# Expert slots dealt out over the partitions in steps of eight, and the last pair's gate and up matrices requested whole

## What is computed

```python
def hier_moe(xn, w_router_group, w_router_expert, w_gate, w_up, w_down):
    t = xn.reshape(-1, D_MODEL)                       # 520 tokens x 1024
    ...
    top_v, top_i = lax.top_k(le_g, TOP_K_IN_GROUP)    # 2 of 32 experts for each token
    ...
    def expert_step(acc, ew):
        wg, wu, wd, cw = ew
        h = jax.nn.silu(t @ wg) * (t @ wu)            # 1024 -> 256
        return acc + cw[:, None] * (h @ wd).astype(jnp.float32), None
```

## Time and profile before

| | us |
|---|---|
| median of 3 runs | 596.83 |
| lowest and highest run | 594.62, 599.33 |
| span of the profiled execution | 599.1 |
| PE busy (share of the span) | 550.2 (92%) |
| DVE busy | 278.3 (46%) |
| ACT busy | 168.1 (28%) |
| POOL busy | 158.0 (26%) |
| queue q1, share of the 16 DMA engines' span | 64.1% |
| queue q0, the same | 7.8% |

### The profile page before, as it was taken

One profiled execution on the slowest core, in us unless ns is written; L12 is line 12 of the kernel. 1 busy time (PEld: TensorE's weight loads), 2 busy tenths in 40 slices (PEclk: granted clock), 3 DMA queues, 4 the chain that ended last, 5 costly groups with the idle time before them and its releaser, 6 DMA issues.

```text
span 599.1 us, 8410 instructions
## 1 busy us (share of the span) xinstructions
PE 550.2 (92%) x2970; PEld 321.9 (54%) x2970; DVE 278.3 (46%) x694; ACT 168.1 (28%) x386; POOL 158.0 (26%) x187
## 2 busy tenths in 40 slices
PE   6999999999999988999999999999996968789994
PEld 4798799897765645554555944333332323234321
DVE  5887677978304799623458531121120111111235
ACT  7445343414302656731322210010110000000013
POOL 0488788410001098610000021111120111101003
PEclk9999999999999999999999798999997989989997
DMA  7890342579575930039905759999999999999966
GB/s 279 275 288 30 121 142 83 181 244 312 190 210 174 400 137 3 3 97 383 401 38 185 307 161 369 408 419 419 420 422 421 420 420 420 421 421 421 381 241 249
DMA packets 48215, 163.48 MB, mean 273 GB/s; under 512 B 8674, under 2 KB 22058, under 8 KB 36888
## 3 DMA queue, kind: packets, MB, share of 16 engines
q1 hardware_dynamic: 41360, 144.93, 64.1%
q0 software_dynamic: 6528, 17.01, 7.8%
q10 hardware_dynamic: 288, 1.05, 0.4%
HBM read 151.06 MB, written 19.76 MB: 285 GB/s over the span
## 4 chain that ended last, share of the span: by engine, by line
PE 48%; DMA 16%; SPq 11%; DVE 7%; POOL 3%; issue 3%; ACT 3%; DVEq 0%; POOLq 0%; ACTq 0%
PE bank L1141 10%; DMA ring<-in_w_up_dram 10%; PE bank L1065 9%; SPq L537 7%; PE bank L1168 4%; DMA x<-q_rows 3%; SPq L550 3%; DMA ring<-results 2%; PE bank L1016 2%; PE bank L930 2%; PE bank L813 2%; PE bank L835 2%; POOL ring L2213 2%; PE bank L836 2%; PE bank L840 2%
## 5 line engine op out<-in xcount | busy, mean ns | idle before, releaser
L1141 PE MATMUL bank<-ring,work 128*64 128x512 f32 x512 | 120.6, 626 | 17.7 <-DMA ring<-in_w_up_dram 17.7
L1141 PEld LDWEIGHTS bank<-ring,work 128*64 128x64 f32 x512 | 39.3, 144 | 95.5 <-issue 82.7
L1518 DVE TENSOR_TENSOR work<-work,bank 128x256 f32<-128x256 f32 x16 | 6.7, 422 | 133.7 <-ACT work L1453 133.7
L756 PE MATMUL bank<-split 128*128 128x384 f32 x192 | 66.1, 344 | 0.1
L1168 PE MATMUL bank<-ring,work 128*64 128x512 f32 x256 | 58.5, 598 | 7.6 <-ACT work L1457 7.6
L757 PE MATMUL bank<-split 128*128 128x384 f32 x192 | 64.3, 335 | 0.0
L2280 POOL DMA_INDIRECT work<-hn_rows,tbl x15 | 15.2, 1016 | 106.5 <-PE bank L1151 91.2
L1065 PE MATMUL bank<-ring 128*128 128x512 f32 x96 | 42.9, 596 | 0.0
L1453 ACT ACTIVATE work<-bank 128x256 f32<-128x256 f32 x16 | 6.2, 384 | 129.7 <-PE bank L1141 129.7
L2288 POOL DMA_INDIRECT results<-work,tbl x15 | 15.0, 1001 | 98.8 <-DVE work L2058 98.8
L2213 POOL TENSOR_TENSOR ring<-ring 128x192 f32<-128x192 f32 (+1 forms) x40 | 38.8, 989 | 8.0 <-DVEq L1613 6.8
(11 more groups left out here) (281 smaller groups left out, 878.9 us busy)
## 6 DMA issues: line engine op xcount, KB each, us to landing
ring<-in_w_down_dram SPq DMA_DIRECT2D x32, 1024.0 KB, 25.0
ring<-in_w_gate_dram SPq DMA_DIRECT2D x28, 1024.0 KB
ring<-in_w_up_dram SPq DMA_DIRECT2D x28, 1024.0 KB
ring<-in_w_in_dram SPq DMA_DIRECT2D x7, 1536.0 KB, 11.3
results<-work POOLq DMA_DIRECT2D x1, 4160.0 KB, 24.5
x<-in_x_prompt_dram SPq DMA_DIRECT2D x8, 512.0 KB, 15.8
ring<-in_w_out_dram SPq DMA_DIRECT2D x2, 2048.0 KB
ring<-in_w_gate_dram SPq DMA_DIRECT2D x8, 512.0 KB, 22.3
```

What stands on the lines that cost most here:

```text
L756: pe.matmul(bank[n % 3][:, 0:CW], xT_high[:, k, cols], w_high[c][:, k, :], start=(k == 0), stop=False)
L1141: last = pe.matmul(bank[2][64 * h:64 * h + 64, :], xgT[:, k, 64 * h:64 * h + 64], gate_up[s][h][:, :, k, :], start=(k == 0), stop=(k == KD ...
L1518: return dve.tensor_tensor(out, a, b, op)
```

## The change

The constant becomes `slot_at`: column p holds the number of the slot that lies on partition p. In each half of 64 partitions, slot 0 is on partition 0, slot 1 on partition 8, and so on to slot 7 on partition 56; slot 8 is on partition 1. `in_order` is a view of the same constant that reads 0 to 127 in order, with a stride of eight, for `holder`. The gathered rows, the results and the one-hot matrices follow the table, so all of them change places together.

For the last pair, SP requests the four gate and up matrices whole by `gates`, all counted on `gu_in[0]`, and PE waits once, for all of them, before the first product. The four requests of 1 MB take the place of eight of 512 KB. The order of the requests (gate and up of expert 30, gate and up of expert 31, then the downs) stays that of the other pairs.

```diff
@@ constants
-    seg["iota128"] = np.tile(p[None], (P, 1))
+    seg["slot_at"] = np.tile((p // SL * SL + p % 8 * 8 + p % SL // 8)[None], (P, 1))
@@ build
-        iota128 = cut(rt, 1472, P)
+        slot_at = cut(rt, 1472, P)
+        in_order = slot_at.rearrange("p (h b a) -> p h a b", h=2, b=8)
@@ SP
-            cseg("iota128", iota128).then_inc(S["logc_in"], 16)
+            cseg("slot_at", slot_at).then_inc(S["logc_in"], 16)
...
             sp.wait_ge(S["gu_done"], PAIRS - 3)
-            half_gates((30, 31), 0, 0, S["front_in"])
-            half_gates((30, 31), 0, 1, gu_in[0])
+            gates((30, 31), 0)
             sp.wait_ge(S["dn_done"], PAIRS - 3)
             downs((30, 31), 0)
@@ PE
-            def pair(i, s, turn, first, split=False):
+            def pair(i, s, turn, first):
...
-                pe.wait_ge(*((S["front_in"], 80) if split else (gu_in[s], loads)))
+                pe.wait_ge(gu_in[s], loads)
                 for k in range(KD):
                     if k == KD // 2:
                         pe.wait_ge(S["xg_evac"], 2 * i + 2)
-                        if split:
-                            pe.wait_ge(gu_in[s], loads)
...
-                pair(i, s, i // 3 + 1, False, i == PAIRS - 1)
+                pair(i, s, i // 3 + 1, False)
@@ DVE, pick and place
-                        dve.tensor_scalar(picked[m][0:n, e * SL:(e + 1) * SL], iota128[0:n, 0:SL], place_in[0:n, m, e:e + 1],
+                        dve.tensor_scalar(picked[m][0:n, e * SL:(e + 1) * SL], slot_at[0:n, 0:SL], place_in[0:n, m, e:e + 1],
...
-                        dve.tensor_scalar(in_slot[:, i, m, :], iota128, slot[:, i, m:m + 1], None, ALU.is_equal)\
+                        dve.tensor_scalar(in_slot[:, i, m, :], slot_at, slot[:, i, m:m + 1], None, ALU.is_equal)\
@@ DVE, pair 14
-                        dve.tensor_scalar(holder[:, t, :], iota128, float(t * P), last_token, ALU.add, ALU.is_equal)\
+                        dve.tensor_scalar(holder[:, t, :].rearrange("p (h a b) -> p h a b", h=2, a=8), in_order,
+                                          float(t * P), last_token, ALU.add, ALU.is_equal)\
```

## The result

The changed kernel takes 608.14 us (median of four runs, 606.99 to 610.83) against 597.34 us for the kernel before (594.62 to 599.33). The ratio is 1.0187 with a 95% interval of 1.0143 to 1.0230, that is 8.5 to 13.7 us more. When both were timed again beside two variants (experiment 7), the ratio was 1.0129 (1.0100 to 1.0158). A ratio is computed from all runs of both kernels, so it differs a little from the quotient of the two medians.

The account below looks back on a forecast made before the run. The expert stage was taken as bound by full DMA engines, the one with most rows setting the end. Slots +11.1 and whole requests +0.4 gave +11.5 us, a median of 608.3 us, range 602.5 to 613.5.

Parts of the forecast that it names:

- Dealing B: Which partitions share a DMA engine: runs of four, the run 32 above on the same one, eight per half.
- the sum: From 371.56 to 575.6 us: 180 us of matrices plus the heaviest engine's rows, together 200.9 of 204 us.
- A and C: Other partition-to-engine dealings: A eight neighbours, C partition mod 16; experiment 4 expected -11.5 us for A, +12 for C.
- The slowest DMA engine sets the end: Expert stage: the DMA engine with most rows sets the end, since every matrix is awaited whole; the tail follows.
- Rival M: In experiment 5: half the DMA engines standing idle costs, not the one with most rows; +3 us or less.
- 11.1 us for part 1: Slots in steps of eight: 61 more rows at 0.156 us on the heaviest engine, 9.5, plus 1.6 for earlier rows.
- Part 2 at +0.4 us: Last pair's gate and up matrices requested whole: +0.4 us, range -0.2 to +1.8.
- the slack: Last pair: PE's products end 3.8 us (tile 3: 2.2) before DVE needs them; starting 2.3 late costs 0 to 0.1.
- Line 2078: DVE's strided read, five instructions of 281 ns: covered by PE's work even at twice the time; uncovered, 1.4 us.
- The faster one: Dealing A, blocks of eight neighbours, makes the new layout the even one: -12.6 us, 584 us; chance 0.04.
- Within 1%: Rows slip in beside matrices, or landings depend less on the slowest engine: +0 to +5 us; chance 0.10.
- The dearest case: Rows at 0.172 us (+13.4), PE's low clock in the tail (+1.8) and pair 14 (+1.7): up to 16.9; chance 0.08.

Follow-up runs that it names:

- experiment 7: The changed kernel itself, timed again beside the kernel before: 606.05 against 598.8 us, ratio 1.0129 (1.0100 to 1.0158).
- experiment 4: Changed kernel with slots dealt in steps of four and the last pair's halves kept, against the kernel before: 596.8 against 598.9 us, ratio 0.9952.
- Experiment 5: Changed kernel with halves kept, slots 0 to 7 on one DMA engine of each half, against the kernel before: 607.4 against 598.5 us, ratio 1.0145.
- experiment 2: Changed kernel with the last pair's matrices in halves again, slots still dealt by eight, against the kernel before: 608.5 against 598.9 us, ratio 1.0146.
- experiment 1: Changed kernel with dense slots again, last pair's gate and up still requested whole, against the kernel before: 598.3 against 598.9 us, ratio 0.9995.
- experiment 6: Changed kernel with filler products on PE before the last pair, against the kernel before: 609.0 against 598.8 us, ratio 1.0185.
- run 32: Not a follow-up run and has no time: the run of four partitions lying 32 higher, served by the same DMA engine.
- experiment 3: Changed kernel with halves kept and slots going round the runs of four, against the kernel before: 596.8 against 598.9 us, ratio 0.9954.

## Why the prediction was right, point by point

**Where a row goes: right.** Dealing B, taken from the spread of 12 us, the burst of 14 DMA engines and the sum, holds. The changed kernel's burst at 205 to 226 GB/s and its plateau at 0.5 were foretold by it, and experiment 4 excludes A and C by their sign and size. The first gather's 14 DMA engines came from a single window of 0.2 us, and this reading was a lucky one: the same 15 or 16 DMA engines show only 205 or 144 GB/s in the windows beside it. The packets in flight, 15 and 10, bear it out. The Trainium skill, "DMA: Bandwidth & Descriptors", section "The descriptor swizzle", states this dealing for one 1 MiB transfer to 128 partitions. The runs agree, for gathers and scatters by an index too.

**The slowest DMA engine sets the end: right.** Experiment 5 shows it without eight crowded DMA engines: two crowded ones cost +8.7 us, as eight do in experiment 2. Rival M, lost bandwidth as such, called for 3 us or less.

**11.1 us for part 1: right within the measurement; the price of a row isn't pinned down.** The stretch grew by 11.8 and 13.1 us in the two profiles of the changed kernel and by 10.9 us with halves, for 61 rows more. Divided by the rows of the stretch alone that is 0.18 to 0.21 us per row (10.9 / 61, 13.1 / 61), and 0.17 with one crowded (11.1 / 66), more than the sum's 0.156 us. But the growth also holds the backlog from the 17 rows ahead of the stretch. Over all 78 rows it is 0.14 to 0.17 us, and 0.13 us over the 84 of the crowded layout. It also holds up to 2.4 us, in experiments 2 and 5, in which the lower clock made PE late to pair 14; the sum had nothing for that. In experiment 7 PE did wait for pair 14's matrices, by 0.45 us. So the 0.156 us is neither confirmed nor refuted, and that the upper bound's 0.172 is the better value isn't shown.

By the timed runs the cost is smaller: +7.7 to +11.2 us by the ratios. That the forecast median, 608.3 us, met the measured 608.14 so closely is luck: the same kernel gave +11.2 us the first time and +7.7 the second, against +11.5 forecast. The profiles of the kernels with crowded DMA engines happened to reach the stretch at 364.9 to 368.6 us, the others at 368.4 to 371.6. At least part of that is chance: two profiles of the changed kernel reach it at 364.9 and 368.6, and they are already that far apart at the first gather (344.06 and 347.73), before any row is gathered by its slot. Whether the rest belongs to the layout is open; nothing ahead of the first gather differs but the constant's values.

**Part 2 at +0.4 us: right in its result, off in its parts.** The ranges of experiments 1, 2 and 7 hold it. The idle time ahead of the last pair, forecast at 2.2 us, was 3.56 and 3.35 us in the changed kernel and 2.80 with dense slots. The step that was off is the slack: the forecast let DVE's gaps absorb the late start, but in all four profiles with a whole request the chain that ended last goes through PE's products (line 1211, or 1213 in experiment 6). At the full clock that cost nothing visible: from the request for the result rows to the end it took 22.5 us in experiment 7, against 23.2 before. At the lower clock it took 24.2 and 24.6 us (changed kernel, experiment 1). The forecast thought the lower clock less likely at 2.2 us of idle time; it was met in two of the three profiles with a whole request and no fillers.

**Line 2078 (now 2076): right.** The strided read costs 45 ns an instruction and lies under PE's work (ns min/median/max, as the earlier trace rows). It is the stride and not the form of the instruction: experiment 1 writes by the same view and reads in a row, at 278 ns.

```profile
L2076 DVE TENSOR_SCALAR work<-rt,st x5: 325/326/327, 567.9 to 568.9; 128x128 f32<-128x128 f32 x5
```

**What was to show it.** The share falls early, the slope is longer than 16 us (24), the waits grow to about 28 us (28.0), the burst is halved. One sign came late: the mean of the stretch up to 556 us fell only from 416 to 410 GB/s, not to 400. It did fall to 401 GB/s from 460 us on (420 before), while the first 89 us stayed at 421. So the lightly loaded DMA engines work ahead through the requests already made at first, and the lost time shows in the second half and in the plateau. That they work ahead is read from these rates; no view shows single DMA engines.

**The rivals.** The faster one (A, 584 us) fell by the result itself and by experiment 4. "Within 1%" fell by the interval, 1.0143 and up; in the second measurement, 1.0100 to 1.0158, it is only just excluded. The dearest case, up to 16.9 us, did not come. Of its three parts, the low clock in the tail was seen in two profiles. A low clock just ahead of pair 14 was seen too, in pair 13's products (8.68 and 8.78 us in the two profiles of the changed kernel, 9.85 in experiment 2, 7.09 before). A dearer row isn't shown.

## What to carry to other kernels

When an indirect DMA moves rows of a tile, a row's DMA engine follows from its partition: here runs of four partitions, and the run 32 higher on the same one, eight DMA engines to each half of 64. If only some rows are real and other transfers fill the queues, count the rows of each DMA engine over the whole stage, and take the largest count, not the mean; a layout that goes round the runs of four is the even one. The sign that it isn't even is a DMA share that runs out in steps at the end of the stage (0.5 for eight of sixteen, 0.12 for two), and a rate that sags ahead of it (401 GB/s for 420) while the mean share still looks full.

## What the runs showed of the hardware

- 61 to 66 rows of 4 KB more on the busiest of the 16 DMA engines made the stretch 10.9 to 13.1 us longer and the timed kernel 7.7 to 11.2 us slower, although the queues held 1 MB requests all the time. By the stretch that is 0.17 to 0.21 us per row, or 0.13 to 0.17 if the rows ahead of the stretch are counted too. Taking 15 rows off it gave 2.8 us by the timed ratio, 1.2 to 1.8 us by the stretch.
- An idle time of PE ahead of a set of products doesn't tell by itself which clock the set meets: after 3.35 us it ran at the full one (7.09 us), after 2.80 and 3.56 us in the same place at the lower (8.78 us). In experiment 7 as little as 2.11 us, ahead of another pair, was followed by the lower clock (granted clock 0.50 in 531.6 to 533.6 us):

```profile
529.61 8.78 PE L1139 MATMUL bank<-ring,work 128*64 128x512 f32 x32 [2.11 <-DMA ring<-in_w_up_dram]
```

- DVE read 128 elements with a stride of eight in 326 ns, with a stride of four in 325 to 328 ns (experiments 3 and 4), and in a row in 278 to 281 ns.
